# The values' compression gets an operand tile of its own, written five chunks earlier, and the pair sums lose their closing zero product

## The reference, cut to what matters

```python
# compress keys and values: windows of 32 tokens, every 16 (15 windows)
def compress(u, pe, w1, w2):
    blk = u[:, tok] + pe[None, None, :, None, :]
    blk = blk.transpose(0, 1, 3, 2, 4).reshape(B, n_cmp, HKV, -1)
    return (jax.nn.silu(blk @ w1) @ w2).transpose(0, 2, 1, 3)
kc = rms_norm(compress(k_cmp, pe_k, w_ck1, w_ck2), g_kc)
vc = compress(v_cmp, pe_v, w_cv1, w_cv2)

# gated linear attention, one chunk of 64 tokens: pair sums with decay
attn = jnp.einsum('bhid,bhjd,bhijd->bhij', qc, kc, decay)
```

## Time and profile before

| | us |
|---|---|
| median of 3 runs | 2412.4 |
| lowest, highest | 2406.01, 2414.59 |
| profiled execution, its own time | 2409.67 |
| its span | 2408.4 |
| TensorE busy | 2395.4 |
| VectorE busy | 1491.3 |
| ScalarE busy | 1122.1 |
| mean granted clock of TensorE | 0.998 |

### The profile page before, as it was taken

How to read it: one execution, slowest core, us unless ns; L and a number is a source line. 1 busy time by engine, 2 the same in 40 slices (tenths; PEclk the granted TensorE clock), 3 DMA queues, 4 the chain that set the end, 5 groups by cost and what they waited for, 6 DMA issues and landing times.

```text
span 2408.4 us, 28130 instructions
## 1 busy us (share of the span) xinstructions
PE 2395.4 (99%) x11328; PEld 1986.7 (82%) x11328; DVE 1491.3 (62%) x2119; ACT 1122.1 (47%) x1410; POOL 0.2 (0%) x4
## 2 busy tenths in 40 slices
PE   9999999999999999999999999999999999999999
PEld 8888888888888888888888887887888888888887
DVE  5565999865544545576667866876555555554443
ACT  5454444544443444454555555546444444444333
POOL 0000000000000000000000000000000000000000
PEclk9999999999999999999999999999999999999999
DMA  7645666656665765666544445554565665566664
GB/s 265 205 143 184 192 192 193 212 192 210 195 193 160 251 228 192 195 215 191 177 149 156 168 139 180 179 181 137 186 192 186 190 192 186 190 192 188 202 203 141
DMA packets 124942, 452.96 MB, mean 188 GB/s; under 512 B 13771, under 2 KB 15996, under 8 KB 123788
## 3 DMA queue, kind: packets, MB, share of 16 engines
q1 hardware_dynamic: 124812, 451.17, 58.1%
HBM read 448.99 MB, written 2.12 MB: 187 GB/s over the span
## 4 chain that ended last, share of the span: by engine, by line
PE 97%; DVE 1%; DMA 1%; ACT 1%; issue 0%; SPq 0%; ACTq 0%
PE ps L1256 30%; PE ps L1258 30%; PE ps L1257 30%; PE ps L773 2%; PE ps L806 1%; PE ps L1118 1%; PE ps L787 1%; DMA t_raw<-w_in 1%; PE ps L797 0%; DVE t_wlo L2490 0%; PE ps L917 0%; PE ps L1288 0%; ACT t_whi L1743 0%; PE ps L1101 0%; PE ps L1022 0%; PE ps L885 0%
## 5 line engine op out<-in xcount | busy, mean ns | idle before, releaser
L2490 DVE TENSOR_TENSOR t_wlo<-t_raw,t_whi 128x1024 fp32r<-128x1024 f32 (+1 forms) x806 | 983.0, 1223 | 802.5 <-ACT t_whi L1743 799.3
L1743 ACT ACTIVATE t_whi<-t_raw 128x1024 fp32r<-128x1024 f32 x804 | 850.0, 1059 | 1016.4 <-PE ps L1258 997.1
L1256 PE MATMUL ps<-t_whi,t_A 128*128 128x512 f32 (+1 forms) x2496 | 986.2, 395 | 2.2 <-DVE t_wlo L2490 2.2
L1258 PE MATMUL ps<-t_wlo,t_A 128*128 128x512 f32 (+1 forms) x2496 | 969.8, 389 | 0.0
L1257 PE MATMUL ps<-t_whi,t_A 128*128 128x512 f32 (+1 forms) x2496 | 968.4, 388 | 0.0
L1256 PEld LDWEIGHTS ps<-t_whi,t_A 128*128 128x128 f32 x2496 | 469.2, 188 | 99.9 <-issue 5.7
L1258 PEld LDWEIGHTS ps<-t_wlo,t_A 128*128 128x128 f32 x2496 | 468.8, 188 | 97.8
L1257 PEld LDWEIGHTS ps<-t_whi,t_A 128*128 128x128 f32 x2496 | 469.5, 188 | 90.9
L1256 PE MATMUL ps<-t_whi,t_Y0a 128*128 128x512 f32 x576 | 225.2, 391 | 0.0
L1258 PE MATMUL ps<-t_wlo,t_Y0a 128*128 128x512 f32 x576 | 224.2, 389 | 0.0
L1257 PE MATMUL ps<-t_whi,t_Y0a 128*128 128x512 f32 x576 | 224.1, 389 | 0.0
(11 more groups left out here) (317 smaller groups left out, 1229.7 us busy)
## 6 DMA issues: line engine op xcount, KB each, us to landing
t_raw<-w_in SPq DMA_DIRECT2D x375, 512.0 KB, 3.9
t_raw<-w_gu SPq DMA_DIRECT2D x176, 512.0 KB, 3.6
t_raw<-w_down SPq DMA_DIRECT2D x88, 512.0 KB, 4.1
t_raw<-w_branch SPq DMA_DIRECT2D x64, 512.0 KB, 4.0
t_raw<-w_out SPq DMA_DIRECT2D x64, 512.0 KB, 3.7
t_raw<-w_ck SPq DMA_DIRECT2D x16, 512.0 KB, 4.1
t_raw<-w_cv SPq DMA_DIRECT2D x16, 512.0 KB, 4.3
t_raw<-w_cq SPq DMA_DIRECT2D x8, 512.0 KB, 3.5
```

The costliest lines, as they stand in the source:

```text
L1256: te.matmul(ps[:, 0:n], u.op.hi[:, x, tok], h[:, k, :], start=(kt == 0), stop=False)
L1258: made = te.matmul(ps[:, 0:n], u.op.hi[:, x, tok], l[:, k, :], start=False, stop=(kt == u.kts - 1))
L1743: se.activation(whi[:, k % NH, 0:n], raw[:, d % NR, 0:n], ACT.Copy).then_inc(*hi.up((d, 1)))
L2490: ve.tensor_tensor(wlo[:, k % NH, p], raw[:, d % NR, p], whi[:, k % NH, p].bitcast(F32), ALU.subtract).then_inc(*lo.up(name))
```

## The change

Three edits go together. `kp` becomes a list `kps` of two tiles: the keys' as before, the values' in the region Y1b, behind `bT`, where the first near tile lay. `compressed` takes the one by the unit's index. The step that writes the values' operand moves from place 49114 to 48614 and waits for `near0.3` instead of the end of ck1; the memset of the two empty columns is made for each tile. Of the pair sums the closing zero product is left out: the last close product has `stop` and raises `pairs`.

```diff
-    compress=[46902, 46914, 46914, 47001, 47001, 49114, 49414, 49600, ...
+    compress=[46902, 46914, 46914, 47001, 47001, 48614, 49414, 49600, ...
...
-    kp = at("Y0b", [32, 32])
+    kps = [at("Y0b", [32, 32]), at("Y1b", [32, 32], off=4096)]
...
-    unit("cv1", dr["w_cv1"], 256, 32, cmp_s["dve"].at("kp_v"), "hid", after=[cmp_s["dve"].at("kcn")], rows=True)
+    unit("cv1", dr["w_cv1"], 256, 32, cmp_s["dve"].at("kp_v"), "hid", after=[cmp_s["dve"].at("kcn")], rows=True,
+         index=1)
...
                 for C, s, a in CLOSE:
+                    done = (C, s, a) == CLOSE[-1]
                     n, p0, i0 = 16 * s, 64 * (C % 2), 64 * C + 16 * s
                     o = i0 if C < 2 else 256 + i0 - P
-                    te.matmul(ps[p0:p0 + n, o:o + 16], kpr[:, a:a + n], q12[:, 1, i0:i0 + 16], start=False, stop=False,
-                              skip_group_check=True)
-                te.matmul(ps[:, 0:384], zer[:, 0:P], zer[:, 0:384], start=False, stop=True,
-                          skip_group_check=True).then_inc(*gla_s["pe"].up(f"pairs{h}"))
+                    made = te.matmul(ps[p0:p0 + n, o:o + 16], kpr[:, a:a + n], q12[:, 1, i0:i0 + 16], start=False,
+                                     stop=done, skip_group_check=True)
+                made.then_inc(*gla_s["pe"].up(f"pairs{h}"))
...
-                made = te.matmul(ps[32 * k:32 * k + 32, 0:u.n], kp[:, kt, :], w[:, k, :], start=(c == 0),
+                made = te.matmul(ps[32 * k:32 * k + 32, 0:u.n], kps[u.index][:, kt, :], w[:, k, :], start=(c == 0),
                                  stop=(c == u.kts // u.per - 1))
...
-        def compress_operand(col, pe_, name):
+        def compress_operand(col, pe_, name, kp):
+            ve.memset(kp[:, :, 30:32], 0.0)
...
-            ve.memset(kp[:, :, 30:32], 0.0)
-            compress_operand(0, par("pe_k"), "kp_k")
-            yield
-            dve.wait_ge(*ended_mm("ck1"))
-            compress_operand(256, par("pe_v"), "kp_v")
+            compress_operand(0, par("pe_k"), "kp_k", kps[0])
+            yield
+            dve.wait_ge(*gla_s["pe"].at("near0.3"))
+            compress_operand(256, par("pe_v"), "kp_v", kps[1])
```

More of the change, by code:

```diff
@@ L90 @@
         47114, 47200, 47201, 47301, 47302],
-    compress=[46902, 46914, 46914, 47001, 47001, 49114, 49414, 49600, 49614, 49700, 49702, 50000, 50101, 50102, 50314,
+    compress=[46902, 46914, 46914, 47001, 47001, 48614, 49414, 49600, 49614, 49700, 49702, 50000, 50101, 50102, 50314,
         50400, 50401, 50801, 50802, 50902, 50914, 51014, 51014, 51102, 51102, 51114, 51114, 51201, 51201, 51202,
```

## The result

The changed kernel takes 2407.81 us in the median of 22 runs (2406.10 to 2410.91), before 2412.41 in the median of 22 (2406.01 to 2414.98). The ratio is 0.9983, with a 95% interval from 0.9977 to 0.9989: 4.6 us or 0.2% faster in the medians. That is inside the 0.5% that the forecast called no change, and with this many runs it is clear of zero. The forecast was 2405.6, range 2400.5 to 2411.0.

The account below looks back on a forecast made before the run. TensorE, busy 99% of the span, was taken to bound the kernel. 1.94 + 2.95 - 0.5 + 0.7 = 5.1 us, off the mean of four executions, 2410.7, gave 2405.6 us; range 2400.5 to 2411.0.

Parts of the forecast that it names:

- The removed and the added wait: VectorE's waits before writing the values' operand, for the end of ck1 and for near0.3: each claimed to cost 0.
- The hole, 1.94 us: TensorE's idle time before chunk 494: operand work moved away starts it 1.94 us earlier, idle time 3.11 to 1.2 us.
- the forecast left 0.3 us the other way: At the old place: the scores' first block claimed ready at about 1457.6, 0.3 us before VectorE comes to them.
- The cover at the new place: At chunk 486: VectorE's added 2.04 us leaves 0.3 us before TensorE's L964 needs L2137's output; cost 0.
- The clock in the hole, 2.95 less 0.5: Behind the hole: clock stays full, so 5.9 us at half clock halves, gain 2.95; 0.5 lost waiting for chunk 496's split.
- The rival that the fall is chance: Clock falls anyway, or by chance in either kernel: gain only 2.6 us, 2407.1 to 2408.1; chance 0.18.
- The zero products, 0.7 us: Pair sums' closing zero product (L1108), four instructions of 384 columns left out: 0.17 us each, gain 0.7, bounds 0 and 1.4.
- the case that the forecast named for its lower bound: Pair sums: gain 0 if the next weight load, hidden under the zero product before, then stands open.
- I find no later hole before 1640: After chunk 496: no later hole that depends on VectorE alone before 1640 us, so only 0.5 us is given back.
- a clock of 0.5 somewhere: Sign of a wrong forecast: the granted clock shows 0.5 anywhere; a right one had 1.00 in the stretch from 1440.
- the two that it names: The 40 us stretches from 1440 and 1640 us, claimed the most idle, with TensorE busy 36.89 and 36.95 us.
- the third rival: Second clock fall, at 1463 and also in the idle time from 1640: 2410.3, slower by 0.6 us; chance 0.05.

Follow-up runs that it names:

- e3: Kernel before, with the values' operand in its own tile and the new wait, still written at old place 49114: 2411.38 us, ratio 0.9999.
- e4: Changed kernel, with VectorE doing the same four additions once more at old place 49114: 2412.66 us, ratio 1.0003 to before.
- e2: Kernel before, with only the closing zero products of the pair sums left out: 2412.55 us, ratio 1.000.
- e6: Changed kernel, with the four additions made twice at new place 48614, first into a spare tile: 2407.89 us, ratio 0.9991 to before.
- e5: Kernel before, with 16 zero products of 384 columns on TensorE between chunks 493 and 494: 2408.22 us, ratio 0.9986.
- e1: Changed kernel, with the closing zero product of the pair sums put back: 2407.85 us, ratio 0.9980 to before.
- e7: Changed kernel, with the 32 narrow score matmuls cut in two, second half behind three wide products: 2406.38 us, ratio 0.9981 to before.
- e11: Changed kernel, with zero products ahead of all 16 scores and the values' operand at place 48814 instead of 48614: 2406.16 us, ratio 0.9977 to before.
- e8: Changed kernel, with a zero product of 272 columns ahead of each of the 16 narrow scores: 2405.44 us, ratio 0.9977 to before.
- e10: Changed kernel, with a zero product of 272 columns ahead of every second narrow score, 8 in all: 2405.15 us, ratio 0.9969 to before.

## Why the forecast was right, and where it wasn't

**The removed and the added wait cost nothing, the place does.** Right: e3 has tile and wait alone and is at 0.9999; e4 puts the work back and loses everything.

**The hole, 1.94 us.** The mechanism is as forecast step by step; in this pair of profiles it shrank by 2.1. But the 3.11 us of before were high. The three other profiles with this work at 49114 and nothing in the hole (e2, e3, e4) have 2.35, 2.40 and 2.36, against 1.00 and 1.01 without it: 1.4 us is the usual size of the term. Two rows say why. In the profile of before the split of chunk 493 began at 1456.75 after a wait of 1.05 us, behind a rounding (L1743) that had waited 0.65 us for its weights:

```profile
1455.66 1.06 ACT L1743 ACTIVATE t_whi<-t_raw 128x1024 fp32r<-128x1024 f32 x1 [0.65 <-DMA t_raw<-w_in]
1456.75 1.23 DVE L2490 TENSOR_TENSOR t_wlo<-t_raw,t_whi 128x1024 fp32r<-128x1024 f32 x1 [1.05 <-ACT t_whi L1743]
```

In the changed kernel it began at 1455.85 after 0.30. And then VectorE is at the scores before they are there: L2375 waited 0.42 for L788, where the forecast left 0.3 us the other way.

**The cover at the new place.** Right, 0.2 us for the 0.3 forecast, and e6 shows the price when it is gone: 1.3 us up to chunk 494.

**The clock in the hole, 2.95 less 0.5.** Right in this pair, 2.4, and both terms are a little smaller than forecast: from the first product of chunk 494 to that of 496 it is 1.97 us instead of 3.01, of which 0.20 is the wait for the split. By e4 against e3 a fall is worth 2.8, and by e5 (ratio 0.9986) the clock is most of the change's gain. The rival that the fall is chance holds for before: hole and clock fell together in three profiles (before, e2, e4) and not in e3. In none of the nine profiles in which the hole was 1.0 us or filled did it fall there. The Trainium skill ("TensorE: Matmul & The Clock Gate", Part 1) says that the monitor runs freely of the kernel and results differ from run to run. The runs agree: one and the same kernel, before, has executions with a mean clock of 0.996 and of 1.000.

**The zero products, 0.7 us.** The mis-sized term: 0.2. Around the first, in the earlier trace rows and the timeline of the changed kernel,

```profile
1241.10 0.50 PE L1257 MATMUL ps<-t_whi,t_A 128*128 128x512 f32 x1
1241.43 0.40 PE L1258 MATMUL ps<-t_whi,t_A 128*128 128x512 f32 x1
```

the step from the first to the second wide product is 0.33 us, where the rate is 0.23. Before, the same two products stood like this:

```profile
1241.28 0.34 PE L1108 MATMUL ps<-t_Y0b 128*128 128x384 bf16 x1
1241.32 0.53 PE L1256 MATMUL ps<-t_whi,t_A 128*128 128x512 f32 x1
1241.69 0.39 PE L1257 MATMUL ps<-t_whi,t_A 128*128 128x512 f32 x1
```

From the start of the zero product to the second wide one it was 0.41 us, which is 0.17 and 0.23 and nothing more; so 0.17 us of columns went and 0.10 us came back, 0.08 in all. The likely cause, which no run isolates, is that a weight load is no longer hidden behind the 384 columns. That is the case that the forecast named for its lower bound, and nearer the truth than its middle; the four together brought 0.21 between 1200 and 1400 us.

**"I find no later hole before 1640".** This step failed, because it looked for holes. There was none, but a fall of the clock with TensorE busy all the time, around the 32 matmuls of 15 columns: 1.7 us lost in the profile. One of the forecast's own signs of being wrong, a clock of 0.5 somewhere, was met by it, and the span is 2405.3 instead of 2403.3. Of the eight profiles that leave the scores as they are, five have the fall (the changed kernel, e1 to e4) and three don't (before, e5, e6). It isn't always at one instruction: in the changed kernel and e1 it came with the last of the 32, in e2 and e4 2.7 us after the first, and in e3 1.2 us behind the last, while L788 ran. Where it lasted longer (e2, e4) it cost 3.3 us. None of the five profiles with zero products or wide products among the scores (e7 to e11) has it.

The mean clocks of all executions say the same. Of the 33 of the changed kernel and of e1 none has a mean clock of 1.000; of the 24 of e8, e10 and e11 there are 15, and these 15 are shorter than the shortest of the 33 (2406.10). The intervals of the ratios overlap, so that the medians are lower by 2.4 and 2.7 us is likely rather than shown; that the fall at the scores is gone in most executions is shown. By what measure the chip decides isn't.

**The sum.** 5.1 us from a profile with one fall of four possible. Profile to profile it was 3.0 (2409.67 to 2406.64), median to median 4.6. The forecast gain is near the second because errors cancel: it took the hole and the zero products too large (by 0.5 and 0.5 us), and it left out both the fall that the changed kernel still has and those that before usually has more of. The mean granted clock is 0.9985 in the 22 executions of the changed kernel and 0.9974 in the 86 of before; 0.0011 of 2408 us is 2.6 us (an estimate), which leaves 2.0 for the hole and the zero products. The time itself, 2407.81, is 2.2 above the forecast, as that started from the mean of four executions, 2410.7, and the median of 22 is 1.7 higher.

Two of the forecast's reasons don't hold. The stretch from 0 us is idle as much as the two that it names (36.92 of 40 us busy), and it isn't touched by the change. The 1640 stretch kept its full clock in the profile of before, but not in e2, e3, e4 and e8, so that one row was no proof for short gaps. One of these, e8, contains the change: the place of the third rival is real, while no run shows that the change makes it more frequent.

Open: the falls at 1207 (e2, e8) and between 1640 and 1648 (e2, e3, e4, e8) weren't worked on. The first comes with TensorE busy too, behind two pairs of matmuls on 16 partitions (L1070 in e2, from 1203.58 and from 1205.52), with three wide products between them; the profile of before has the same matmuls and no fall there.

## What to carry to other kernels

When a kernel is 99% TensorE, its medians can still differ by what the clock does in a few places, and one profile shows one draw of it: take the granted clock in windows from several profiles, and the mean clock of every execution, before a term of the sum rests on it. Work on an in-order engine that nobody needs soon belongs ahead of a wait that the engine has anyway, not ahead of what TensorE waits for. Where TensorE must wait, or has only narrow matmuls, try a few wide zero products; here 8 of them at the scores gave the lowest median, 2405.15 us in 5 runs against 2407.81.

## What the runs showed of the hardware

TensorE's clock fell to 1.2 GHz without any idle time of TensorE, during or up to 1.2 us behind 32 fp32 matmuls of 15 columns, and in the changed kernel the eight matmuls behind them took 3.2 us instead of 1.6. With a hole of 2.4 us it fell in one execution (e4) and not in another (e3). The kernel before alone takes from 2406.0 to 2415.8 us, and its mean granted clock goes from 1.000 to 0.996 with it. A bf16 zero product of 384 columns in front of a wide product cost 0.05 us, 16 of 272 columns between narrow fp32 matmuls 0.5 us together (32 narrow ones take 3.6 us alone and 4.1 with the 16 among them).
